# Second feed-forward of a fused two-block program: seven quarter products for eight, hidden activations through DRAM, the down products in a stage of their own

## The reference, cut to what matters

```python
def swiglu(h, w_gate_up, w_down):          # h [1024, 1024], w_gate_up [1024, 2*2816], w_down [2816, 1024]
    gu = h @ w_gate_up
    gate, up = jnp.split(gu, 2, axis=-1)
    return (jax.nn.silu(gate) * up) @ w_down

hs = hs + rms_norm(swiglu(rms_norm(hs, g_pre), w_gate_up[1], w_down[1]), g_post)
```

## Time and profile before

| what | value |
|---|---|
| runs of the kernel before | 2837.12, 2831.42, 2828.78 us |
| span of the profiled execution | 2827.2 us |
| PE busy | 2655.4 us, 94% of the span |
| VectorE busy | 1234.2 us, 44% |
| ScalarE busy | 782.9 us, 28% |
| GpSimd busy | 248.0 us, 9% |
| first matmul of f1 to last VectorE write of its tail | 1275.5 to 2042.7 us of the span |
| median us from issue to landing, 512 KB of w_gate_up | 5.7 |
| the same, 512 KB of w_down | 3.3 |

### The profile page before, as it was taken

One profiled execution on the slowest core, in us unless ns is written; L12 is line 12 of the kernel. 1 busy time (PEld: TensorE's weight loads), 2 busy tenths in 40 slices (PEclk: granted clock), 3 DMA queues, 4 the chain that ended last, 5 costly groups with the idle time before them and its releaser, 6 DMA issues. The chain is left out here.

```text
span 2827.2 us, 47951 instructions
## 1 busy us (share of the span) xinstructions
PE 2655.4 (94%) x20165; PEld 2210.2 (78%) x20165; DVE 1234.2 (44%) x2074; ACT 782.9 (28%) x1483; POOL 248.0 (9%) x175
## 2 busy tenths in 40 slices
PE   9899999999998999989999999999799999688778
PEld 8899999999986866667888888887677777577656
DVE  6433333333334458462333333333624464444366
ACT  6321111111126249442121111111322422233231
POOL 2100000000002025100000000000600000222110
PEclk9999999999998999999999999999899999899979
DMA  6311111111114500322111111111310211100132
GB/s 181 98 45 45 45 45 45 45 45 45 45 60 166 187 35 2 97 104 86 45 45 49 60 47 45 45 45 54 134 58 26 97 53 67 44 5 4 42 118 93
DMA packets 62950, 183.52 MB, mean 65 GB/s; under 512 B 10581, under 2 KB 19062, under 8 KB 61246
## 3 DMA queue, kind: packets, MB, share of 16 engines
q1 hardware_dynamic: 62784, 181.12, 19.1%
HBM read 150.48 MB, written 30.03 MB: 64 GB/s over the span
## 5 line engine op out<-in xcount | busy, mean ns | idle before, releaser
L812 DVE TENSOR_TENSOR f1hf<-f1sg,f1gu 128x512 f32<-128x512 f32 x44 | 30.3, 688 | 336.9 <-ACT f1sg L759 336.9
L812 DVE TENSOR_TENSOR f0hf<-f0sg,f0gu 128x346 f32<-128x346 f32 (+1 forms) x66 | 34.1, 517 | 327.6 <-ACT f0sg L759 327.6
L860 PE MATMUL f0gu<-b1XH,f0w0H 128*128 128x346 f32 (+1 forms) x528 | 170.5, 323 | 4.7 <-DVE f0w0L L792 4.1
L823 DVE TENSOR_TENSOR Y<-f0dn,Y 128x512 f32<-128x512 f32 (+1 forms) x180 | 124.0, 689 | 113.7 <-PE f0dn L907 112.7
L862 PE MATMUL f0gu<-b1XH,f0w0L 128*128 128x346 f32 (+1 forms) x528 | 171.1, 324 | 0.0
L861 PE MATMUL f0gu<-b1XL,f0w0H 128*128 128x346 f32 (+1 forms) x528 | 170.5, 323 | 0.0
L862 PE MATMUL f0gu<-b1XH,f0w1L 128*128 128x346 f32 (+1 forms) x528 | 170.2, 322 | 0.0
L861 PE MATMUL f0gu<-b1XL,f0w1H 128*128 128x346 f32 (+1 forms) x528 | 169.7, 321 | 0.0
L860 PE MATMUL f0gu<-b1XH,f0w1H 128*128 128x346 f32 (+1 forms) x528 | 169.0, 320 | 0.0
L823 DVE TENSOR_TENSOR Y<-f1dn,Y 128x512 f32<-128x512 f32 x160 | 109.3, 690 | 88.8 <-PE f1dn L907 88.8
L860 PE MATMUL f1gu<-b1XH,f1w0H 128*128 128x512 f32 x352 | 139.5, 396 | 3.2 <-DVE f1w0L L792 3.2
(11 more groups left out here) (430 smaller groups left out, 6605.8 us busy)
## 6 DMA issues: line engine op xcount, KB each, us to landing
f0raw<-in_w_gate_up SPq DMA_DIRECT2D x43, 512.0 KB, 5.8
f1raw<-in_w_gate_up SPq DMA_DIRECT2D x43, 512.0 KB, 5.7
residual<-Y SPq DMA_DIRECT2D x32, 512.0 KB, 2.8
Y<-in_w_ada SPq DMA_DIRECT2D x8, 1536.0 KB, 6.4
f0rawd<-in_w_down SPq DMA_DIRECT2D x22, 512.0 KB, 3.2
f1rawd<-in_w_down SPq DMA_DIRECT2D x22, 512.0 KB, 3.3
w_in_b_raw<-in_w_in_b SPq DMA_DIRECT2D x16, 512.0 KB, 3.3
w_in_a_raw<-in_w_in SPq DMA_DIRECT2D x11, 512.0 KB, 4.2
```

Of the source, the lines that this page charges most:

```text
L812: dve.tensor_tensor(hf[:, i, 0:w], sg[:, i, 0:w], gu[:, i, 1, 0:w], ALU.mult).then_inc(s["mul"], 1)
L823: dve.tensor_tensor(y, dn[0:r, (par * ND + i) % 4], y, ALU.add).then_inc(s["acc"], 1)
L860: pe.matmul(o, wH[c][:, j, k], xh, start=(k == 0), stop=False)
```

## The change

`strassen_ffn` takes the place of `ffn_stage` for f1 (not for f0). It has two stages.

**Gate and up.** The two first chunks are made as before (96 matmuls each). For each of the other 20 chunks, the product [gate; up] times X is cut in quarters: the weights by gate or up and by the lower or upper 512 input features, X by the input features and by the two halves of 512 tokens. Seven products of sums of quarters (4 blocks deep, 3 matmuls: 12 matmuls each, 84 per chunk) stand for the eight (96). The sums of X's quarters (S1, S3, S4, and S2 in the place of one quarter of XH and XL) are made once, by VectorE, while PE makes the first two chunks. For each chunk VectorE makes four weight sums (three instructions, 2048 elements a partition), ScalarE and VectorE split 7 pieces of 512 for 8 (four instructions each), and results are carried between three PSUM banks by ScalarE copies into the tile tm and VectorE adds (three each per chunk). The hidden chunk, gate times up, is no longer split at once: SP stores it to DRAM (`hidden`, two stores of 256 KB a chunk).

**Down.** 77 steps, seven products (P1, P5, P6, P3, P7, P2, P4) of 11 steps. A step is one hidden chunk or sum of chunks [128 x 512 tokens] and one block or sum of blocks of w_down [128 x 512 features]: 4 token tiles of 3 matmuls, 12 matmuls. What a step needs is loaded from DRAM into a ring of five slots (or kept: KA, KS, KB), summed by VectorE, copied by ScalarE and subtracted by VectorE. A product's four results stay in PSUM over its 11 steps, and over the next product on the same banks; in between they are copied to Y (12 ScalarE copies) or added to Y (12 VectorE adds). The last five steps of P4 go tile by tile.

The tail is the same class, with the transposes in four of the banks, lag_h 2 for 3 and lag_l 3 for 4. The first four token tiles go through it while P4 is made: its pieces stand in front of steps 71 to 74 in ScalarE's and VectorE's lists, in PE's list behind steps 69, 70, 71 and the third tile of the last five steps, and in SP's list behind the loads of steps 71 to 74. Y is no longer cleared by GpSimd.

The diff, cut to its core (the call, the loads, sums and splits of a step, and the lists of the engines in the down stage, HQ is 11, OUTER 72; the second table is that of the sums):

```diff
-            ffn_stage(b, lambda sp: b.fetch_first(sp, ins["w_in_2"][0:P, 512:1024]), "f1", 1, TILES_SEQ, SLICES_SEQ, 3, lambda ctx, ready: Tail(
-                b, ctx, "p3", TILES_SEQ, lambda t: x3[P * t:P * (t + 1), :], x4, ins["norm_ffn_post"][1], modulate=(scale1, shift), lag_2=1, lag_h=3, lag_l=4, ready=ready))
+            strassen_ffn(b, lambda sp: b.fetch_first(sp, ins["w_in_2"][0:P, 512:1024]), "f1", 1, 0, 1, lambda ctx, ready, tp: Tail(
+                b, ctx, "p3", TILES_SEQ, lambda t: x3[P * t:P * (t + 1), :], x4, ins["norm_ffn_post"][1], modulate=(scale1, shift), lag_2=1, lag_h=2, lag_l=3, ready=ready, tp=tp))
...
+    R = 5
+    HQ = HALF_Q
...
+        ORDER = ("P1", "P5", "P6", "P3", "P7", "P2", "P4")
+        steps = [(p, j) for p in ORDER for j in range(HQ)]
+        AHEAD = 4
...
+        def loads(n):
+            p, j = steps[n]
+            r = n % R
+            ra, rb = (ring_plain[:, r, x] for x in range(2))
+            sa, sb_ = stg[0][:, r], stg[1][:, r]
+            k2 = HQ + j
+            if p == "P1":
+                if j < R:
+                    return [(ra, hidden_tiles(j, 0)), (rb, down(j, 0))]
+                more = [(KB[:, j - R], down(j - R, 0))] if j < 2 * R else []
+                return [(ra, hidden_tiles(j, 0)), (KB[:, j], down(j, 0))] + more
+            return {
+                "P5": [(sa, hidden_tiles(j, 1)), (KS[:, j], hidden_tiles(k2, 1)), (sb_, down(j, 1))],
+                "P6": [(KA[:, j], hidden_tiles(j, 0)), (sa, down(k2, 1))],
+                "P3": [(ra, hidden_tiles(k2, 0)), (rb, down(k2, 1))],
+                "P7": [(sa, hidden_tiles(j, 1)), (rb, down(k2, 1)), (sb_, down(j, 1))],
+                "P2": [(ra, hidden_tiles(k2, 0)), (rb, down(k2, 0))],
+                "P4": [(ra, hidden_tiles(k2, 1)), (rb, down(k2, 0))],
+            }[p]
...
+            return {
+                "P1": [],
+                "P5": [(KS[:, j], KS[:, j], sa, ALU.add), (KB[:, j], sb_, KB[:, j], ALU.subtract)],
+                "P6": [(KS[:, j], KS[:, j], KA[:, j], ALU.subtract), (KB[:, j], sa, KB[:, j], ALU.subtract)],
+                "P3": [(ra, ra, KS[:, j], ALU.subtract)],
+                "P7": [(ra, KA[:, j], sa, ALU.subtract), (rb, rb, sb_, ALU.subtract)],
+                "P2": [],
+                "P4": [(rb, rb, KB[:, j], ALU.subtract)],
+            }[p]
...
+        P4_FIRST = 6 * HQ
+        EARLY = FIRST_TILE + 4
+        OUTER = P4_FIRST + HQ - R
...
+                def step_loads(n):
+                    if n >= R:
+                        sp.wait_ge(s["pd"], 4 * (n - R + 1))
+                    for dst, a in loads(n):
+                        sp.dma_start(dst, a).then_inc(s_ld[n % R], 16)
...
+                kept = 0
+                for n in range(P4_FIRST, len(steps)):
+                    step_loads(n)
+                    if n >= P4_FIRST + R - FIRST_TILE and kept < EARLY:
+                        tail.keep(sp, kept)
+                        tail.load(sp, kept + tail.loads)
+                        kept += 1
...
+                def step_high(n):
+                    p = steps[n][0]
+                    if sums(n):
+                        act.wait_ge(s["ad"], made[n + 1])
+                    act.wait_ge(s_ld[n % R], landed_at[n])
+                    for x, a in sources(n):
+                        act.activation(ring[:, n % R, 2 + x.start:2 + x.stop], a, ACT.Copy).then_inc(s["h2"], 1)
...
+                def step_low(n):
+                    todo = sums(n)
+                    dve.wait_ge(s_ld[n % R], landed_at[n])
+                    for dst, x, y, op in todo:
+                        dve.tensor_tensor(dst, x, y, op).then_inc(s["ad"], 1)
+                    at_h = split_at[n]
+                    for x, a in sources(n):
+                        at_h += 1
+                        dve.wait_ge(s["h2"], at_h)
+                        dve.tensor_tensor(ring[:, n % R, x], a, ring[:, n % R, 2 + x.start:2 + x.stop].bitcast(f32), ALU.subtract).then_inc(s["l2"], 1)
...
+                done = {4 * HQ + AHEAD: (4 * HQ - 1, bank_b, 0, 1, 8), 5 * HQ + AHEAD: (5 * HQ - 1, bank_a, 1, 1, 4), 6 * HQ + AHEAD: (6 * HQ - 1, bank_b, 0, 0, 0)}
+                tails = 0
+                for n in range(len(steps)):
+                    if n in done:
+                        add_out(*done[n])
+                    if n >= P4_FIRST + R - FIRST_TILE and tails < EARLY:
+                        tail.vector(dve, tails)
+                        tails += 1
+                    step_low(n)
...
+                for n in range(OUTER):
+                    p, j = steps[n]
+                    pe.wait_ge(s["l2"], split_at[n + 1])
+                    for t in range(4):
+                        if j == 0:
+                            emptied(p, t)
+                        bank = (bank_b if p in ("P5", "P3", "P2") else bank_a)[t]
+                        tile(n, t, bank, j == 0 and p in ("P1", "P5", "P2"), j == HQ - 1).then_inc(s["pd"], 1)
...
+                    if n >= OUTER - 3 - FIRST_TILE:
+                        tail.tensor(pe, n - (OUTER - 3 - FIRST_TILE))
+                pe.wait_ge(s["l2"], split_at[-1])
+                for t in range(4):
+                    for n in range(OUTER, len(steps)):
+                        mm = tile(n, t, bank_a[t], False, n == len(steps) - 1)
+                    mm.then_inc(s["pd"], 1)
+                    if t == 2:
+                        tail.tensor(pe, EARLY - 1)
```

More of the change, by code:

```diff
@@ L152, in __init__ @@
         self.fetched = 0
+        with ExitStack() as rounded:
+            self.Y_rounded = self.sb(rounded, "Y_rounded", [P, (NT + 1) * D], f32r)
         self.Y = self.sb(ctx, "Y", [P, NT + 1, D])
@@ L196, in alloc_x @@
     def alloc_x(self, ctx, name, tokens, side="left"):
+        with ExitStack() as plain:
+            self.XH_plain = self.sb(plain, name + "XH_plain", [P, KC, tokens], f32, side)
+            self.XL_plain = self.sb(plain, name + "XL_plain", [P, KC, tokens], f32, side)
         self.XH = self.sb(ctx, name + "XH", [P, KC, tokens], f32r, side)
@@ L474, in __init__ @@
     def __init__(self, b, ctx, name, tiles, residual, store, post_gain, pre_gain=None, modulate=None, cols=None,
-                 ready=None, junk=None, sole=False, loads=2, slots=2, lag_2=2, lag_h=3, lag_l=None):
+                 ready=None, junk=None, tp=None, sole=False, loads=2, slots=2, lag_2=2, lag_h=3, lag_l=None):
         self.b, self.tiles, self.residual, self.store = b, tiles, residual, store
@@ L490, in __init__ @@
         self.st = b.sb(ctx, name + "st", [P, 6, 9])
-        self.tp = b.ps(ctx, name + "tp", [P, slots, KC, P])
+        self.tp = tp if tp is not None else b.ps(ctx, name + "tp", [P, slots, KC, P])
         names = [f"rx{i}" for i in range(loads)] + ["gains", "ss1", "sd1", "r1", "xg", "x", "ss2", "sd2", "r2", "xn", "tp", "xh", "xl", "stored"]
```

558 lines of the change are left out of this document (added).

## The result

The median of the changed kernel is 2803.7 us (2801.6 to 2806.7) and that of the kernel before 2832.3 us (2828.8 to 2837.1) in the same comparison: ratio 0.99, 95% interval 0.9885 to 0.9915. The forecast was 2806. The profiled execution has a span of 2799.8 us for 2827.2 before.

A forecast was written before the change was run, and what follows sets the result against it. TensorE's matmul count was taken to bound f1; 433.4 + 2.0 + 1.0 + 2.9 + 213.9 + 19.8 + 44.5 + 20.6 + 4.0 = 742.1 us for 767.2, 25.1 less, giving 2806 us; main-case range 2780 to 2830.

The forecast's parts named there:

- gate and up with cold start: Gate and up: 1872 matmuls at 0.2315 us, 433.4 us, plus 2.0 cold and 1.0 for the start.
- change of stage: Between gate and up and down: PE idle 2.9 us behind the last silu, a copy and a subtraction.
- P1 to P2, 66 steps: Down before P4: 2.78 us a step, plus 19.8 us of stalls where the VectorE-ScalarE chain outlasts PE's step.
- P4 and early tail, cold matmuls in it: Last product with first tail tiles: 44.5 us of waits and transposes, plus 4 us of matmuls at 1.2 GHz.
- behind the last matmul: Tail after f1's last matmul: 20.6 us for 17.8 before, two tiles queuing for GpSimd and VectorE.
- The carries through PSUM: Gate and up: costed at nothing under another bank's product; without that cover about 0.7 us each, six a chunk.
- The lead for P5: VectorE's head start entering P5: 3.1 us, paying for all but 1.6 of P5's 4.7 us of stalls.
- Loads bind: Rival, P1 to P2: 256 KB loads at 1.5 us each set the pace, some 55 us more, 2861; 9%.
- The clock falls: Rival, P5 to P7: short PE stops bring 1.2 GHz, 36 steps lose 1.9 us each, 68 us, 2874; 3%.
- the clock term: P4: 4 us added for matmuls at 1.2 GHz behind waits of 9 to 13 us.
- All is hidden: Rival: VectorE's lead covers the chains and the early tail finds gaps; 86.1 us less, 2745; 4%.
- The exclusion: P4 and tail: VectorE instructions with both inputs in SBUF and GpSimd exclude each other; without it about 14 us less.

The follow-up runs named there:

- e2: Changed kernel with no tail tile begun before P4's last five steps and all transposes after the last matmul; 2803.6 us, ratio 0.9893.
- e3: Changed kernel with one more 256 KB load that nobody reads in every step of P6, P3 and P2; 2808.5 us, ratio 0.9911.
- e1: Changed kernel with VectorE making the next step's sums before it waits for ScalarE's copy of this one; 2793.2 us, ratio 0.9845.
- e7: Changed kernel with next-step sums issued ahead, the tail's loads spread over steps, and the tail's GpSimd additions on VectorE; 2777.1 us, ratio 0.9806.
- e8: Changed kernel with down made of 88 plain steps in place of the 77 of seven products; 2802.6 us, ratio 0.9911.
- e4: Changed kernel with everything on the right side of SBUF shifted by 32 bytes; 2796.3 us, ratio 0.9861.

## Why the prediction was right

The mechanism and its sum held; f1 came out 5 us shorter than forecast and the later stages 3 longer. That the total is off by so little is in part luck: terms below miss by up to 7 us and cancel, and the code behind f1 alone varies by 6 us from kernel to kernel. By the forecast's own terms:

| term | forecast, us | measured, us |
|---|---|---|
| gate and up with cold start | 436.4 | 434.1 |
| change of stage | 2.9 | 2.96 |
| P1 to P2, 66 steps | 203.3 | 204.0 |
| P4 and early tail, cold matmuls in it | 79.1 | 77.4 |
| behind the last matmul | 20.6 | 18.7 |
| sum | 742.3 | 737.2 |

- **Gate and up.** The carries through PSUM cost nothing, as argued: PE is busy 100.0 of 100.0 us in the first window, and has no wait up to 1710.0. The rest is a matmul's interval that is 0.2267 on some operands (below), not 0.2315.
- **The change of stage** cost what the three instructions in a row gave, 2.96.
- **The steps.** Periods forecast 3.20, 2.95 and 3.55; measured 3.20, 2.95 and 3.56. An unstalled step takes 2.72 and not 2.78, and the stalls come to 24.5 us, not 19.8. The two misses cancel, since VectorE's period sets the time of a step from P5 to P7 and a faster PE only waits longer. The lead for P5 was given 3.1 us; P5 is 3.3 over its steps, P6 5.0, P3 3.2, P7 10.9, and P1, which starts cold, and P2 make up the other 2.1.
- **P4.** The first wait is 13.14 for 13.5. The waits behind it sum to 20.3 us where I had 27.4, and transposes with cold matmuls take 14.0 (77.4 less 33.5 of waits and 29.9 of steps) where 3.6 and 4.0 were written: the clock term was mis-sized, the windows show 0.78 and 0.70 there, and matmuls behind such waits start 0.43 us apart. With the shorter steps (0.7) these cancel to 1.7. What e2 adds: without these PE waits f1 is only 1.4 us shorter, since the tail's work comes later instead.
- **Behind the last matmul.** The queue of tiles in GpSimd and VectorE was there, 18.7 for 20.6.
- **The rivals.** *Loads bind* is wrong for the steps, by e3. But the prediction costed the tail's six loads only within this rival (as six of 512 KB, where one is 256 KB), and had no place for their bunching; e1 shows that place, worth 7 us as soon as the chain is shorter. *The clock falls* is wrong for waits of half a microsecond: granted clock 1.00 in the windows of P5, P6 and P3, and in P7 only the wait of 2.90 us was followed by cold matmuls. The rival was priced over 36 steps; the four products have 44. The Trainium skill (TensorE: Matmul & The Clock Gate, "A second HAM failure mode: psum-queue depth-cycling") warns of such short idles; these windows don't show it. *All is hidden* would have needed e7's order of work and a free tail; e7 is still 32 us above its 2745.
- **The exclusion.** The rule that only instructions with both inputs in SBUF exclude held: in P4 a sum (L1465) took 2.83 us beside GpSimd and 1.97 another time for 0.68 alone, while L611, with one input in PSUM, took 1.22 inside an addition of GpSimd (1955.33). The prediction put 14 us on it. That size was not tested without moving work; giving VectorE the additions returned 4.9.

The timeline of VectorE and of GpSimd in P4 of the changed kernel, for the last point:

```profile
1939.69 1.97 DVE L1465 TENSOR_TENSOR f1ring_plain<-f1ring_plain,f1kb 128x512 f32<-128x512 f32 x1 [3.08 <-DMA f1ring_plain<-in_w_down]
...
1946.75 2.83 DVE L1465 TENSOR_TENSOR f1ring_plain<-f1ring_plain,f1kb 128x512 f32<-128x512 f32 x1
...
1938.78 2.33 POOL L548 TENSOR_TENSOR p3xn<-p3xn,p3shift 128x1024 f32<-128x1024 f32 x1
1945.84 3.19 POOL L543 TENSOR_TENSOR Y<-Y,p3rx 128x1024 f32<-128x1024 f32 x1 [4.74 <-DVE Y L590]
```

The sum of 1946.75 ends at 1949.58, and GpSimd's addition at 1949.03: the sum could only run when that was over.

What the prediction did not ask is which part of the change earns the gain. e8 answers for down: its 132 matmuls less (30.6 us) were spent on the chain, the adds and the early tail. With seven products in gate and up alone (240 matmuls less, 55.6 us) f1 is 743.9 us for 769.5 before (2044.96 - 1275.51), 25.5 less. The other 30 us, 6 of them the bunch, go with the move of down into a stage of its own, which e8 keeps; no run has the seven products of gate and up beside the old down, so what these would give in that arrangement is open.

## What to carry to other kernels

When fewer matmuls are bought with sums on another engine, write down the period of the chain sum, copy, low part: if it is above PE's step, the saving stays on paper until the next step's sums are issued ahead of the wait. After each such repair look at the queues again, for a bunch of large loads that the slower chain covered becomes the next wait. And before a long wait of PE is counted as a cost, ask who ends the stage: here the last matmul came 34 us earlier and the stage ended 1.4 us earlier.

## What was not expected of the hardware

The interval between matmuls depends on what the moving operand is. The timeline of PE in gate and up of the changed kernel, the end of a product that reads the sums (sx) and the start of one that reads XH and XL:

```profile
1424.09 0.39 PE L1494 MATMUL f1ps<-f1sx,Y_rounded 128*128 128x512 f32 x1
1424.32 0.39 PE L1495 MATMUL f1ps<-f1sx,Y_rounded 128*128 128x512 f32 x1
1424.54 0.39 PE L1496 MATMUL f1ps<-f1sx,Y_rounded 128*128 128x512 f32 x1
1424.77 0.40 PE L1494 MATMUL f1ps<-b1XH,Y_rounded 128*128 128x512 f32 x1
1425.01 0.39 PE L1495 MATMUL f1ps<-b1XL,Y_rounded 128*128 128x512 f32 x1
1425.24 0.40 PE L1496 MATMUL f1ps<-b1XH,Y_rounded 128*128 128x512 f32 x1
```

Twelve with sx take 1422.05 to 1424.77, 2.72 us; those with XH and XL start 0.2333 apart, 2.80 for twelve. The ring of the down stage is at 2.72 too. Shape and type are the same, and the granted clock is 1.00 from 1376 to 1710. e4 shows that 32 bytes of shift move the last stage from one interval to the other and gate and up hardly at all; what decides stays open.
